# A two-block transformer kernel: new order of the projection's products, and norm splits woven into the product behind them

## What is computed

```python
hl = modulate(rms_norm_2(x_lat, norm1_g[l]), sh1, sc1)      # shift and scale from the conditioning
p = hl @ P["w_in"]                                          # gate part a, queries, keys, values, filter part c
q = qk_heads(p[..., COL_Q:COL_K], P["q_norm_g"], rope)      # root-mean-square norm per head, rotation
k = qk_heads(p[..., COL_K:COL_V], P["k_norm_g"], rope)
a, g = jnp.split(pc, 2, axis=-1)                            # filter part
y = dwconv(a * jax.nn.sigmoid(g), P["conv_w"], P["conv_b"]) # 31 taps along the tokens, 256 channels
o = blocked_diff_attn(q, k_all, v_all, lam)                 # two softmaxes per head, subtracted
x_lat = x_lat + g1 * mixer_merge(pa, o, pc, P, lam_init)    # @ w_out
h2 = modulate(rms_norm_2(x_lat, norm2_g[l]), sh2, sc2)
x_lat = x_lat + g2 * conv_ffn(h2, P)                        # w_gate, 3 taps, silu, w_val, w_down
```

## Time and profile before

| what | us |
|---|---|
| median of 3 runs | 2446.95 (2436.7 to 2447.53) |
| profiled execution, device time | 2444.05 |
| its span, first to last instruction | 2442.4 |
| TensorE busy in the span | 2222.0 (91%) |
| VectorE busy | 1421.3 (58%) |
| ScalarE busy | 1063.3 (44%) |
| GpSimd busy | 304.7 (12%) |

### The profile page before, as it was taken

One profiled execution on the slowest core, in us unless ns is written; L12 is line 12 of the kernel. 1 busy time (PEld: TensorE's weight loads), 2 busy tenths in 40 slices (PEclk: granted clock), 3 DMA queues, 4 the chain that ended last, 5 costly groups with the idle time before them and its releaser, 6 DMA issues. The chain is left out here.

```text
span 2442.4 us, 31205 instructions
## 1 busy us (share of the span) xinstructions
PE 2222.0 (91%) x11948; PEld 1803.7 (74%) x11948; DVE 1421.3 (58%) x2234; ACT 1063.3 (44%) x1753; POOL 304.7 (12%) x310
## 2 busy tenths in 40 slices
PE   8998999899999989899999797789999998778999
PEld 6776677778777766777787675567888886658987
DVE  4655485554456555755454598755555337866664
ACT  4444555444344434554444454523232225454342
POOL 0007121100000062221000073100000001500000
PEclk9998999999999989999999898789999999889999
DMA  7553334466556534345656321222333334234654
GB/s 234 185 179 133 117 129 142 157 214 203 199 188 210 167 118 142 97 144 175 236 170 192 130 69 52 70 69 70 104 129 97 124 99 147 69 105 131 202 174 149
DMA packets 171842, 349.28 MB, mean 143 GB/s; under 512 B 11824, under 2 KB 23216, under 8 KB 171696
## 3 DMA queue, kind: packets, MB, share of 16 engines
q1 hardware_dynamic: 171696, 347.29, 43.7%
HBM read 346.19 MB, written 1.05 MB: 142 GB/s over the span
## 5 line engine op out<-in xcount | busy, mean ns | idle before, releaser
L820 DVE TENSOR_TENSOR wlo<-wraw,whi 128x1024 fp32r<-128x1024 f32 (+1 forms) x538 | 646.0, 1214 | 712.9 <-ACT whi L1017 710.9
L1017 ACT ACTIVATE whi<-wraw 128x1024 fp32r<-128x1024 f32 (+1 forms) x552 | 557.7, 1026 | 603.7 <-PE psum L1773 280.0
L1773 PE MATMUL psum<-whi,act_h 128*128 128x512 f32 (+2 forms) x1424 | 578.7, 406 | 30.4 <-DVE wlo L820 21.8
L1773 PE MATMUL psum<-wlo,act_h 128*128 128x512 f32 (+2 forms) x1424 | 557.4, 391 | 0.0
L1773 PE MATMUL psum<-whi,act_l 128*128 128x512 f32 (+2 forms) x1424 | 557.1, 391 | 0.0
L1773 PEld LDWEIGHTS psum<-whi,act_h 128*128 128x128 f32 x1424 | 275.6, 194 | 100.2 <-DVE wlo L820 25.6
L1773 PEld LDWEIGHTS psum<-whi,act_l 128*128 128x128 f32 x1424 | 274.4, 193 | 57.7
L1773 PEld LDWEIGHTS psum<-wlo,act_h 128*128 128x128 f32 x1424 | 275.4, 193 | 48.7
L1773 PE MATMUL psum<-act_h,whi 128*128 128x512 f32 (+1 forms) x704 | 243.8, 346 | 14.8 <-DVE cacc L1395 6.3
L1773 PE MATMUL psum<-act_l,whi 128*128 128x512 f32 (+1 forms) x704 | 239.6, 340 | 0.0
L1773 PE MATMUL psum<-act_h,wlo 128*128 128x512 f32 (+1 forms) x704 | 239.1, 340 | 0.0
(11 more groups left out here) (268 smaller groups left out, 2772.8 us busy)
## 6 DMA issues: line engine op xcount, KB each, us to landing
wraw<-in_w_in SPq DMA_DIRECT2D x136, 512.0 KB, 4.4
wraw<-in_w_gate SPq DMA_DIRECT2D x104, 512.0 KB, 4.2
wraw<-in_w_mod_pieces SPq DMA_DIRECT2D x96, 512.0 KB, 4.7
wraw<-in_w_ffn_in SPq DMA_DIRECT2D x80, 512.0 KB, 4.4
wraw<-in_w_ffn_out SPq DMA_DIRECT2D x44, 512.0 KB, 4.1
wraw<-in_w_down SPq DMA_DIRECT2D x44, 512.0 KB, 4.3
wraw<-in_w_val SPq DMA_DIRECT2D x40, 512.0 KB, 4.2
wraw<-in_w_branch SPq DMA_DIRECT2D x32, 512.0 KB, 4.8
```

The lines of the kernel that those rows point to most:

```text
L820: eng.tensor_tensor(wlo[:, i, 0:st.n, 0:st.w], wraw[:, st.s % RING_W, 0:st.n, 0:st.w], whi[:, i, 0:st.n, 0:st.w].bitcast(F32), ALU.subtrac ...
L1017: nc.scalar.activation(whi[:, d % RING_S, 0:st.n, 0:st.w], wraw[:, s % RING_W, 0:st.n, 0:st.w], ACT.Copy).then_inc(sem("slab_rounded"), 1)
L1773: return nc.tensor.matmul(out, lhsT, rhs, start=start, stop=stop)
```

## The change

It does five things, all in the second block.

1. The projection's products come in the order q, k, c, a, v. The numbers `at` of the woven steps move: the sums of q from 8 to 4 and of k from 13 to 9, `cglu` from 5 to 13, `cT` from 6 to 14, the taps from 7, 7, 11, 12, 12, 17, 17, 18 to 14, 15, 15, 16, 17, 17, 18, 19, `qkT2` from 18 to 16, the gelu and the norm of a one slab later.
2. The eight splits of each norm are woven into the first product behind it: four ahead of slab 0, two behind slab 0, two behind slab 1.
3. The splits of the mixer output are woven the same way into the product with `w_out`, whose first group now takes its slabs in the order of the splits (rows 0, 6, 2, 4).
4. The bank counter is set to 0 ahead of the feed-forward, so that its first group stands on banks 0 to 3.
5. In the attention, `subln` and its two parts come behind the transposes, exponentials and mix of the same turn of the loop, no longer between `att2_v` and `att2_t`.

```diff
-def gemm(pl, weight, layer, act, tiles, nk, col0, width, evac, row0=0, kt0=0, ready=(), turned=False, **more):
+def gemm(pl, weight, layer, act, tiles, nk, col0, width, evac, row0=0, kt0=0, ready=(), turned=False, order=None, **more):
...
+    order = order or range(0, nk, SLAB_K)
...
-        for k in range(0, nk, SLAB_K):
+        for at, k in enumerate(order):
             n = min(SLAB_K, nk - k)
-            last = k + n == nk
+            last = at == len(order) - 1
...
-            pl.steps += ss
-            return {st.k: [("mod_lo", st.lo)] for st in ss}
-
-        ready = norm(0, 4, l > 0)
+            return {st.k: [("mod_lo", st.lo)] for st in ss}, between(ss)
+
+        def between(ss):
+
+            return [(0, st) for st in ss[:4]] + [(1, st) for st in ss[4:6]] + [(2, st) for st in ss[6:]]
+
+        ready, ss = norm(0, 4, l > 0)
...
-        gc = project(C_C, T, ready)
-        gq = project(C_Q, T)
+        gq = project(C_Q, T, ready)
         gk = project(C_K, 4)
+        gc = project(C_C, T)
         ga = project(0, T)
         gv = project(C_V, 4)
...
-        for i, (g, tiles, at) in enumerate(((gq, T, 8), (gk, 4, 13))):
+        for i, (g, tiles, at) in enumerate(((gq, T, 4), (gk, 4, 9))):
...
-        others = [(5, cglu), (6, ct)] + [(at, st) for at, st in zip((7, 7, 11, 12, 12, 17, 17, 18), parts)]
-        others += qk + [(17, gelu), (18, qkt), (18, aln[0]), (19, aln[1])]
+        others = ss + [(13, cglu), (14, ct)] + [(at, st) for at, st in zip((14, 15, 15, 16, 17, 17, 18, 19), parts)]
+        others += qk + [(18, gelu), (16, qkt), (19, aln[0]), (20, aln[1])]
         others.sort(key=lambda v: v[0])
-        pl.steps += weave(gc + gq + gk + ga + gv, others)
+        pl.steps += weave(gq + gk + gc + ga + gv, others)
...
+            behind = []
...
                 if kind == "att2_v":
-                    att += pending[:1]
+                    behind += pending[:1]
                     del pending[:1]
...
-                        att.append(subs[-1])
+                        behind.append(subs[-1])
...
+            att += behind
...
-        pl.steps += ss
-
-        def residual(weight, act, nk, g, ready, summed):
-            out = gemm(pl, weight, l, act, T, nk, 0, D, "res", ready=ready, g=g)
+
+        def residual(weight, act, nk, g, ready, summed, others=(), order=None):
+            out = gemm(pl, weight, l, act, T, nk, 0, D, "res", ready=ready, g=g, order=order)
...
-            pl.steps += out
-
-        residual("w_out_2", "act2", KD, 0, {st.k: drained(st.bank) for st in ss}, True)
-
-
-        ready = norm(1, T, True)
+            pl.steps += weave(out, others)
+
+        residual("w_out_2", "act2", KD, 0, {st.k: drained(st.bank) for st in ss}, True, between(ss), order[::SLAB_K])
+
+
+        ready, ss = norm(1, T, True)
...
-        pl.turns = tuple(range(7))
+        pl.turns, pl.gemm_banks = tuple(range(7)), 0
...
-                pl.steps += gemm(pl, weight, l, "act2", T, KD, a, w, evac, ready=ready, turned=True, n0=n0)
-                ready = ()
+                pl.steps += weave(gemm(pl, weight, l, "act2", T, KD, a, w, evac, ready=ready, turned=True, n0=n0), ss)
+                ready = ss = ()
```

More of the change, by code:

```diff
@@ L171, in gemm @@
             banks.append(pl.gemm_bank())
-        for k in range(0, nk, SLAB_K):
+        for at, k in enumerate(order):
             n = min(SLAB_K, nk - k)
-            last = k + n == nk
+            last = at == len(order) - 1
             st = Step(kind="slab", s=len(pl.slabs), weight=weight, layer=layer, row=row0 + k, n=n, col=col0 + a, w=w,
-                      act=act, kt=kt0 + k, tiles=tiles, banks=banks, first=k == 0, last=last, c=c, a=a, evac=evac,
+                      act=act, kt=kt0 + k, tiles=tiles, banks=banks, first=at == 0, last=last, c=c, a=a, evac=evac,
                       turned=turned, **more)
@@ L181, in gemm @@
                 st.ready = [w for i in range(n) for w in ready.get(k + i, [])]
-            elif c == 0 and k == 0:
+            elif c == 0 and at == 0:
                 st.ready = list(ready)
@@ L197, in gemm @@
             elif (pl.mod_queue or pl.mod_last) and tiles == 2 and st.s >= 3 * RING_W:
-                at, slabs_in = k // SLAB_K, -(-nk // SLAB_K)
-                if pl.mod_queue and at % 4 == 0 and at + 3 < slabs_in:
+                if pl.mod_queue and at % 4 == 0 and at + 3 < len(order):
                     st.after = mod_ride(pl, pl.next_bank())
```

## The result

The changed kernel takes 2451.08 us (median of 17 runs, 2444.31 to 2462.83); in the same comparison the kernel before takes 2437.89 (17 runs, 2429.39 to 2447.53). The ratio is 1.0054, with a 95% interval of 1.0042 to 1.0067: 13 us slower (10 to 16), just over the 0.5% that the prediction took as its bound, which the interval includes. The forecast's 2450.0 rested on a median of 2446.95 for the kernel before, which the longer comparison puts at 2437.89. So the number came out and the difference did not: +2.5 was forecast on the profiled execution, +13 is measured. That 2450.0 lies 1 us from 2451.08 is luck, for the base that it stands on was 9 us too high. The profiled execution after takes 2458.16, its span is 2456.5, 14.1 more than before.

The account below looks back on a forecast made before the run. TensorE, 91% busy, was taken as the bound, with VectorE's queue ending last in the projections. Terms +4 +2 +0.5 -5.5 +3 -0.5 +2 -3 = +2.5 on 2444.05 gave 2449.5, called 2450; range 2421 to 2467.

Parts of the forecast that it names:

- What bounds the kernel: Whole kernel: TensorE works 91% of the span, so only its waits and half-clock stretches can be won.
- Waits in the projections: Projections: key-scaling waits of 16.5 and 11.6 us go; waits of 15 and 12 come at q and k's transposes.
- Price of a tap: VectorE in the projections: a tap beside GpSimd's additions takes 1.5 us in layer 0, 0.82 in layer 1.
- about 1511: Layer 0's projection: VectorE ends the gelu part's norm then, so attention's first product starts at 1511 against 1507.0, +4 us.
- A break: Woven norms: TensorE pays about 2.5 us behind slabs 0 and 1 with four tiles, 1.4 with two.
- +3.4: Layer 0's first norm: two breaks cost 5.0 us, the earlier slab 0 wins 1.6; net loss 3.4.
- rival (b): Half clock lasts 10 us into work behind each wait or break, so the kernel takes 2467 us; chance 0.20.
- 8.2 + 2.3 - 5.0 = 5.5 won: Layer 0's feed-forward: slab 0 starts 8.2 us earlier, full clock wins 2.3, two breaks cost 5.0.
- Layer 1's feed-forward, "+2": Layer 1's two-tile second norm: two breaks of 1.4 us, 1 won, +2; banks had not held slab 0.
- w_out and the attention's order: Mixer output: +0.5 us in layer 0, -0.5 in layer 1; attention: squares moved behind ScalarE's copies, -3 us.
- Rival (a): VectorE keeps up in the projections: taps cost 0.77 and 0.5 us, 30 us less, 2420; chance 0.22.
- (c): Parts cancel further: breaks of 1 us, a tap of 1.4, some 8 us less, 2442; chance 0.08.

Follow-up runs that it names:

- short_adds: Kernel with only the new projection order, GpSimd's 30 additions cut to 8 columns per sequence; 2408.37 us, 0.9874 of the kernel before.
- own_step: Changed kernel with every odd block's subtraction issued in its own step, block 1 ahead of slab 0 included; 2430.93 us, 0.9968 of the kernel before.
- banks_alone: Kernel before with only the bank counter set to 0 ahead of both feed-forwards, splits unwoven; 2433.21 us, 0.9978 of the kernel before.
- flush: Changed kernel with the subtractions of blocks 3 and 5 issued in their own steps; 2442.21 us, 1.0011 of the kernel before.
- weave_alone: Kernel before with only both norms' splits woven and the feed-forward's bank counter set to 0; 2450.23 us, 1.0059 of the kernel before.
- qkt_last: Changed kernel with the transposes of q and k moved behind the last value slab; 2449.45 us, 1.0040 of the kernel before.

## Why the prediction was right and wrong, point by point

- **What bounds the kernel: right.** Nearly all of the change lies in TensorE's idle time (13.3 of 14.1 us); busy times are the same within 5 us.
- **Waits in the projections: right in place, near in size.** 15 and 12 us were forecast at the transposes of q and k; 14.2 and 9.5 came. That VectorE's copy ends the wait was wrong for its first part, which ScalarE's copy ends.
- **Price of a tap: right.** 1.5 and 0.82 were taken, 1.55 and 0.81 (medians) came, and short_adds shows the cause. By the Trainium skill (SBUF — State Buffer, Who interferes with whom) this is the lock that was cited; the slabs' subtractions, with two inputs as well, agree: 2.25 us beside additions. The same rule should have been applied to them: two ahead of the copies of q and k cost 4.5, where "two slab subtractions (1.22 each)" counted 2.4. But this did not move the copies, for the 16 taps ahead of them took 22.3 and not 24.0 (the first is a plain scaling of 0.55): from the first tap to the copies it is 26.5 us, as forecast (26.4). Layer 0's projection lost 7.8 and not 4 in other places. Half clock in the norm put the taps' start 1.5 us late (1449.8 for 1447.7, of which 0.65 is the later start of the norm in this execution). The four copies of VectorE, two of which wait for TensorE's transposes, took from 1476.3 to 1480.6, where the forecast has one of 0.7 and leaves the others unnamed (its written terms, 1474.8 + 2.4 + 22.5 + 8.8, make 1508.5 and not "about 1511"). And the last 15 taps took 24.4 for 22.5. So the norm ended at 1515.4.
- **A break: right, 2.39 us for 2.5** with four tiles, 2.4 and 2.7 in layer 1's projection, and 1.45 for 1.4 with two. **"+3.4" in the norm of layer 0 was mis-sized:** 5.0 came. Between the two lies 3.4 us of half clock over slab 0, 1.7 us, which the forecast put at zero, and for which it had rival (b).
- **"8.2 + 2.3 - 5.0 = 5.5 won" in layer 0's feed-forward: the wrong term is the 2.3**, the gain of a slab 0 at full clock. Slab 0 ran 5.7 us at half clock, longer than the 4.67 before; 2.5 came (1.8 over the stage). own_step and banks_alone show what was there to be won: 8 to 9 us, given back in two breaks and half clock.
- **Layer 1's feed-forward, "+2": right for the splits (2.3), but a term is missing.** The counter that frees layer 0's first group puts layer 1's w_down on the banks of the last value group: 2.5 us. The prediction looked at the first group that the new count serves and not at the last.
- **w_out and the attention's order: right in size, wrong in the way.** -3 was forecast, the parts alone gave -3.9 (0 to -7.6). But the term was built from ScalarE's copies for TensorE, 5.7 us of waits of which 0.8 for each of four tiles should go, and these waits rose to 8.3 us. The gain came with the waits for VectorE's mix, 8.3 to 2.8 in layer 0 and 4.7 to 1.9 in layer 1, to which the prediction gave no part in it. That its size fits is luck.
- **Rival (a)** fell, since a tap is 1.55 us. Its condition made true (short_adds) gave 37 us against its 30. **Rival (b)** was half true: half clock over the first slabs of the four norms cost 8.6 us (half of 3.4, 5.7, 3.5 and 4.5) against 4.2 before; it had 10 more. **(c)** fell.
- **The forecast missed the main point.** It called the woven norm a loss and sized it near enough, yet did not weigh that it would outdo the order in every stage: three of its four norms lose, 11 us, and the fourth gains less than its banks do. Taken alone, the weave costs 18 to 20, the banks give 5, the order costs 2 to 11 by its ratio, the attention gives 4. That the total stayed within the forecast's range says little for the sum: its terms had a loss of 2.5 where 13 came.

## What to carry to other kernels

Whoever weaves producers between the steps of their consumer must look at software pipelines inside the producer: a subtraction that lags one block behind cost nothing here while blocks followed each other, and 1.36 us of TensorE's time wherever the chain was cut. Cut the chain only where nothing lags, here one line worth 20 us, and compare with not weaving at all, which was as fast here. Shift a bank counter only after looking at the last user it meets as well as the first. And where one queue ends last, move out of it what is needed late, then check whether the stage that takes it in had room: layer 1's had, layer 0's had not.

## What the runs showed of the hardware that was not expected

- With a stop of TensorE of 1.0 to 1.3 us behind the transposes of four-tile splits (own_step) half clock ended 2.9 to 4.0 us behind the first transpose. With stops of 1.9 to 2.2 us there it ended at 9 to 11.4 in five of the six four-tile norms of the changed kernel and flush, in two of them (layer 0's projections) after a spell of full clock in between, and at 4.4 in the sixth; in weave_alone and qkt_last it ended at 8.8 to 11.7 in all six. About a microsecond of stop went with up to 3 us of lost work. With two tiles it made no difference: 7.6 us after a stop of 0.8 (own_step), 7.9 after one of 1.4 (the changed kernel).
- GpSimd's addition keeps VectorE's taps at 1.5 us only while it is long itself: on 16 columns it takes 0.59 us and the tap 0.75, as alone. Shortening an addition by 1 us gave VectorE 0.75 back.
- Executions of one kernel spread by up to 23 us, and the profiled executions differ by up to 7 us ahead of the change (the first norm of the second block starts anywhere from 1349.4 to 1356.5 us in these kernels, whose first block is the same). Stages cut at common events were the steadier measure: layer 0's norm and projection take 152.5 to 153.1 us in the five kernels that have them as before.
